# RWKV block inverse with the identity added to its scores; work of the next chunk spread over other levels; a new order at the end of the S5 part

## The reference, cut to what matters

```python
def step(state, inp):                       # wkv7, 8 heads of 64
    r_t, w_t, k_t, v_t, z_t, b_t = inp
    sa = jnp.einsum('bhvk,bhk->bhv', state, z_t)
    state = (state * w_t[:, :, None, :] + sa[..., None] * b_t[:, :, None, :]
             + v_t[..., None] * k_t[:, :, None, :])
    return state, jnp.einsum('bhvk,bhk->bhv', state, r_t)
...
_, _, st_re, st_im = lax.associative_scan(_cplx_op, (a_re, a_im, bu_re, bu_im), axis=1)   # odd_mixer, S5
y = (jnp.einsum('gcn,bsgn->bsgc', C_re, st_re) - jnp.einsum('gcn,bsgn->bsgc', C_im, st_im))
y = jax.nn.gelu(y + D * u)
val, gate = jnp.split(y @ w_glu, 2, axis=-1)
return val * jax.nn.sigmoid(gate)
```

## Time and profile before

| | |
|---|---|
| median of 3 runs | 2760.04 us |
| profiled execution, its own time | 2760.72 us |
| its span | 2758.5 us |
| mean granted TensorE clock | 0.977 |
| TensorE busy | 2622.4 us, 95% of the span, 13567 instructions |
| VectorE, ScalarE, GpSimd busy | 1301.3, 934.0, 879.3 us |
| chain that ended last, by engine | PE 62%, issue 5%, DVE 2%, POOL 2%, ACT 1% |

### The profile page before, as it was taken

How to read it: one execution, slowest core, us unless ns; L and a number is a source line. 1 busy time by engine, 2 the same in 40 slices (tenths; PEclk the granted TensorE clock), 3 DMA queues, 4 the chain that set the end, 5 groups by cost and what they waited for, 6 DMA issues and landing times.

```text
span 2758.5 us, 35785 instructions
## 1 busy us (share of the span) xinstructions
PE 2622.4 (95%) x13567; PEld 2180.1 (79%) x13567; DVE 1301.3 (47%) x1572; ACT 934.0 (34%) x1420; POOL 879.3 (32%) x781
## 2 busy tenths in 40 slices
PE   6999799999799999999999999979999999999998
PEld 4778588888577887888788888868878888888886
DVE  5532277676434556564564435642244413431443
ACT  3442354454433322343343334412233212221333
POOL 4222234333232223575572221222222222222221
PEclk7999899999899999999999999989999999999999
DMA  2111000000012211243251134621111111111112
GB/s 86 44 46 49 20 1 1 1 1 1 13 45 58 58 44 58 64 144 106 65 175 58 46 99 163 202 79 50 47 41 49 50 50 46 49 49 46 49 46 84
DMA packets 239923, 164.57 MB, mean 60 GB/s; under 512 B 23981, under 2 KB 227271, under 8 KB 237767
## 3 DMA queue, kind: packets, MB, share of 16 engines
q1 hardware_dynamic: 225344, 141.37, 17.1%
q10 hardware_dynamic: 14471, 21.74, 2.2%
HBM read 129.51 MB, written 29.36 MB: 58 GB/s over the span
## 4 chain that ended last, share of the span: by engine, by line
PE 62%; issue 5%; DVE 2%; POOL 2%; ACT 1%; DMA 0%; ACTq 0%; SPq 0%; POOLq 0%; DVEq 0%
PE acc_o L1556 53%; PE acc_o L1805 4%; POOL dense_lo L374 1%; PE bank_a L2705 1%; PE bank_b L2728 1%; PE bank_b L2458 1%; PE bank_b L2463 1%; PE bank_a L2449 1%; POOL c_lo L2567 0%; DVE val L2038 0%; PE acc_o L2105 0%; POOL t_gx L2381 0%; POOL t_mg L2374 0%; DVE fine L2222 0%; ACT u_now L2807 0%
## 5 line engine op out<-in xcount | busy, mean ns | idle before, releaser
L374 POOL TENSOR_TENSOR dense_lo<-dense_raw,dense_hi 128x512 fp32r<-128x512 f32 x324 | 427.7, 1320 | 1200.4 <-ACT dense_hi L367 1199.1
L367 ACT CAST dense_hi<-dense_raw 128x512 fp32r<-128x512 f32 x324 | 192.4, 594 | 778.3 <-PE acc_o L1556 719.2
L1556 PE MATMUL acc_o<-a_hi,dense_hi 128*128 128x512 f32 x1328 | 413.9, 393 | 8.2 <-POOL a_lo L2573 4.6
L1556 PE MATMUL acc_o<-a_hi,dense_lo 128*128 128x512 f32 x1328 | 410.7, 391 | 0.0
L1556 PE MATMUL acc_o<-a_lo,dense_hi 128*128 128x512 f32 x1328 | 410.5, 390 | 0.0
L1556 PE MATMUL acc_o<-c_hi,dense_hi 128*128 128x512 f32 x1096 | 340.1, 392 | 22.9 <-POOL dense_lo L374 20.7
L1556 PE MATMUL acc_o<-c_lo,dense_hi 128*128 128x512 f32 x1096 | 338.2, 390 | 0.0
L1556 PE MATMUL acc_o<-c_hi,dense_lo 128*128 128x512 f32 x1096 | 338.1, 390 | 0.0
L1556 PEld LDWEIGHTS acc_o<-a_hi,dense_hi 128*128 128x128 f32 x1328 | 247.2, 189 | 62.1 <-POOL a_lo L2573 5.8
L1556 PEld LDWEIGHTS acc_o<-a_hi,dense_lo 128*128 128x128 f32 x1328 | 250.2, 188 | 52.5
L1556 PEld LDWEIGHTS acc_o<-a_lo,dense_hi 128*128 128x128 f32 x1328 | 250.1, 188 | 52.5
(11 more groups left out here) (382 smaller groups left out, 3776.4 us busy)
## 6 DMA issues: line engine op xcount, KB each, us to landing
dense_raw<-in_f_w_up SPq DMA_DIRECT2D x176, 256.0 KB, 3.0
dense_raw<-in_f_w_down SPq DMA_DIRECT2D x72, 256.0 KB, 2.9
w_raw_e<-in_e_w_in SPq DMA_DIRECT2D x44, 256.0 KB, 2.9
s_states<-t_hx ACTq DMA_DIRECT2D x16, 512.0 KB, 3.0
g_in<-s_inputs SPq DMA_DIRECT2D x8, 1024.0 KB, 5.0
hx<-s_states SPq DMA_DIRECT2D x8, 1024.0 KB, 5.3
dense_raw<-in_o_w_glu SPq DMA_DIRECT2D x32, 256.0 KB, 2.8
s_inputs<-t_in ACTq DMA_DIRECT2D x14, 512.0 KB, 2.7
```

The lines of the kernel that those rows point to most:

```text
L367: nc.scalar.copy(self.hi[:, par, 0:n, :], self.raw[:, par, 0:n, :]).then_inc(w_hi_done, 1)
L374: pool.tensor_tensor(self.lo[:, par, 0:n, :], self.raw[:, par, 0:n, :], self.hi[:, par, 0:n, :].bitcast(F32), op=ALU.subtract).then_inc(w_ ...
L1556: last = nc.tensor.matmul(acc[:, h * HALF:(h + 1) * HALF], w[:, chunk, j, :], x[:, k + j, h * HALF:(h + 1) * HALF], start=first, stop=final)
```

## The change

Part one, the inverse. To the masks of levels 1 to 6 and to `a_zb` the identity is added. A product of (A + I) with X, masked, then has ones on its diagonal, and X times it already contains the old X. The products with the identity (`old`) and the additions (`add_old`) go; VectorE copies group 1 out of PSUM. `a_zb` is now an addition on GpSimd, ahead of `first_pool`.

Part two, the order. `roots_act` becomes `logs_act` behind level 3 and `roots_act` behind level 4; the second pair of exponentials moves behind level 5; `zr_dve` to level 6, `r_dve` behind all levels; `b_pool` ahead of `out_pool`.

Part three, the end of the S5 part. The first six places of the GLU's weights are written out as a table of unit and half; a third unit begins in `bank_a`, which the S5 part no longer needs by then. `states_pe(7)` stands ahead of `output_pe(6)`. All eight `g_part` are on VectorE, four of them ahead of scan 6. Moves of tile 5 are split between SyncE's and ScalarE's queues.

```diff
@@ masks, one instruction
+                    link.run(nc.vector.tensor_tensor(level_mask[:, 1:LEVELS, :], level_mask[:, 1:LEVELS, :],
+                                                     ident[:, :].unsqueeze(1).to_broadcast([P, LEVELS - 1, P]), ALU.add))
@@ close_pe
-                up(add4(banks[g][1], x_inv_t[g], MX_AT[g], None if g else x_inv[g]), f"x_ps{g}")
-                up(add4(banks[g][2], mx[g], XT_AT[g], None if g else x_inv_t[g]), f"x_ps{g}")
+                up(add4(banks[g][1], x_inv_t[g], MX_AT[g]), f"x_ps{g}")
+                up(add4(banks[g][2], mx[g], XT_AT[g]), f"x_ps{g}")
@@ close_dve
-            add_old(c, x_inv[1][:, :, :], banks[1][1], "x1")
+            up(nc.vector.tensor_copy(x_inv[1][:, :, :], psum4(banks[1][1])), "x1")
@@ a_zb
-                up(nc.scalar.copy(a_zb[g][:, :, :], a_b[g][:, :, 0, :]), "a_zb")
+                ptt(pool, a_zb[g][:, :, :], a_b[g][:, :, 0, :],
+                    ident[:, :].unsqueeze(1).to_broadcast([P, RT, CH]), ALU.add, "a_zb")
@@ turn_of_act
-                if k == 3:
+                if k in (3, 4):
+                    half = logs_act if k == 3 else roots_act
...
                 if more and k == 4:
                     exps_act(act, c + 1, 1 - s, 0)
+                if more and k == 5:
                     exps_act(act, c + 1, 1 - s, 1)
@@ S5 end, TensorE
                 states_pe(DT - 2)
-                unit_products(dn, pe, DT, a_hi, a_lo, u_glu, 0, 0, g_ready)
+                pe.wait_ge(unit_free, u_glu + 1)
+                place_products(pe, 0, 0, 2, g_ready)
                 filters_pe(DT - 2)
...
+                states_pe(DT - 1)
+                place_products(pe, 0, 2, 4, g_ready).then_inc(w_used, 1)
                 output_pe(DT - 2)
...
+                place_products(pe, 1, 0, 4, g_ready).then_inc(w_used, 1)
                 filters_pe(DT - 1)
                 output_pe(DT - 1)
...
+                place_products(pe, 2, 0, 4, g_ready).then_inc(w_used, 1)
+                place_products(pe, 3, 4, 8, g_ready).then_inc(w_used, 1)
+                place_products(pe, 4, 4, 8, g_ready).then_inc(w_used, 1)
+                place_products(pe, 5, 4, 8, g_ready).then_inc(w_used, 1)
@@ S5 end, SyncE
                 move_y(sp, DT - 2, (2, 3))
                 move_y(sp, DT - 1, (2, 3))
-                with sp.Fori(1, DT) as i:
+                load_unit(DT + 2)
+                dn.load(sp, w_glu, DT, glu_cols(1, 1), u_glu + 3, 0)
+                with sp.Fori(2, DT) as i:
```

More of the change, by code:

```diff
@@ L952, in grow_pe, with add4 @@
                 up(last, f"mx_ps{g}")
-        def add4(bank, lhs, rhs_at, old=None):
-            if old is not None:
-                units(bank, eye, old, start=True, stop=False)
+        def add4(bank, lhs, rhs_at):
             for i in range(RT):
-                last = beside_zeros(bank, i, lhs[:, i, :], rhs_at + i, start=old is None and i == 0, stop=i == RT - 1)
+                last = beside_zeros(bank, i, lhs[:, i, :], rhs_at + i, start=i == 0, stop=i == RT - 1)
             return last
@@ L2104, in tile_products @@
             for h in range(2):
[L2105 removed]
+                last = nc.tensor.matmul(acc[:, h * HALF:(h + 1) * HALF], w[:, place, j, :],
                                         x[:, k, h * HALF:(h + 1) * HALF], start=first, stop=final)
```

183 lines of the change are left out of this document (110 added, 73 removed).

## The result

| | before | after |
|---|---|---|
| median | 2760.56 us (4 runs, 2758.92 to 2761.87) | 2726.47 us (4 runs, 2726.26 to 2726.75) |
| ratio | | 0.9879, 95% interval 0.9864 to 0.9893 |
| span of the profiled execution | 2758.5 us | 2724.5 us |
| granted TensorE clock | 0.977 | 0.981 |

34.1 us less where 35 was forecast, at 2726.5 for a forecast of 2725. The total hides an error. The table follows the same instructions through the two profiled executions; the lead is what the kernel after has won by then.

A forecast was written before the change was run, and what follows sets the result against it. With TensorE at 95% of the span, its waits and what it executes were the question. RWKV 14.7 plus S5 end 20.5, 35.2 us off 2760.7, gave 2725 on the median; own range 2719 to 2731, 8 in 10 2707 to 2740.

The forecast's parts named there:

- RWKV, what goes: Levels 1 to 6 of a chunk: copies through the identity and waits for roots and z go, 4.3 us per full chunk.
- The collision d: Start of a chunk: GpSimd's a_zb additions and VectorE's first masks exclude each other, costing 2.0 us; bounds 0 and 2.5.
- Chunks 0 and 7: First and last RWKV chunk: levels gain only 2.3 and 2.6 us, less d: 0.3 and 0.6.
- S5, the wait for g_in: Before states 7 TensorE waits from 1791.9 to 1792.6; g_in, issued after four moves, takes 5.0 us to land.
- S5, the two later waits: TensorE idles 3.4 us before the last tile and 2.7 before unit 3, whose weights wait in ScalarE's queue.
- One clock fall, 2.5 us: S5 end: idle lowers TensorE's clock; one fall charged at about 2.5 us, bounds none and two.
- Scan 6: VectorE at the S5 end: with GpSimd silent, scan 6 takes 11 us instead of 19.3.
- No collision: Rival on the first masks: d is 0, RWKV gives 31 us, total 2709; chance 0.22.
- VectorE paces the levels: Rival: the 0.46s are lost to evictions, RWKV gives 0 to 3 us, total 2739; chance 0.15.
- The S5 end gives half, g_in lands late and the clock drops: Rival: g_in later among the moves, both idles drop the clock; 11 us there, total 2734; chance 0.13.
- The slower rival: Clock falls inside RWKV through waits in the levels, for more than one chunk's worth: 2765 to 2800; chance 0.03.
- That the copies had no price: Rival: products may overlap the identity copies, so only the ordering acts; falls together with the second rival, no own chance.

The follow-up runs named there:

- The halves measured alone: Kernel before with only the RWKV parts (inverse and order): 2743.53 us, 16.9 less; with only the new S5 end: 2746.73 us, 13.7 less.
- Experiment 5: Changed kernel with GpSimd's two a_zb additions waiting for VectorE's two first masks instead of the kept scores: 2714.38 us, 12.1 less than the changed kernel.
- experiment 6: Changed kernel with g_in of the last group read ahead of states 6 and the last places' weights in SyncE's queue: 2723.61 us, 2.9 less.
- experiment 8: Changed kernel with the hi part of unit 3's first weights ahead of the first output tile on ScalarE: 2722.23 us, 4.2 less.
- experiment 7: Changed kernel with the last weight loads ahead of the last tile's moves in SyncE's queue: 2726.21 us, against 2726.47.
- experiment 3: Inverse without the new order, S5 end as before, against the kernel before: 2765.6 us, 5.2 slower, ratio 1.0022.
- experiment 9: Changed kernel with the GpSimd wait, g_in first, last weights ahead of moves and unit 3's rounding first, all four: 2704.29 us, 22.2 less.

## Why the prediction was right, and where it was wrong

**The number was right in part by luck.** RWKV gave 14.8 us for 14.7, the S5 end 6.2 less than its 20.5, and 4.9 us that belong to no part of the change filled most of the gap: 2.5 ahead of chunk 0, 0.9 between RWKV and states 6, 1.5 at the sums of the last norm. In the first place the code differs by one more instruction on the masks, in the other two by nothing, and the rows differ by the clock: the four products of L319 at 45 us took 3.75 us before and 2.35 after, three pairs at 1076.8 took 1.06 each before and 0.62 after, the norm's sums 3.42 and 1.91. In the 14 traces chunk 0 begins between 340.80 and 343.94 us, and the changed kernel's is the earliest. The halves measured alone, with less of this luck, gave 16.9 and 13.7. How the executions without a trace divide is not shown.

- *RWKV, what goes (4.3 a chunk).* It was 4.44, all of it in the levels 1 to 6. Step by step, each level counted from its first product or copy, with the forecast in brackets: 0.00 (-0.1), -0.46 (-0.45), -0.47 (-0.45), -1.37 (-1.35), -1.69 (-1.5), -0.45 (-0.4). The chunk period is 47.60 for the 48 named. The level without filler is 3.67, as forecast. VectorE's copy costs what its addition did (a pair takes 1.29 us in both traces).
- *The collision d (2.0).* The mechanism was right and the size nearly: 1.78. Experiment 5 shows it. The row that the prediction gives as s_prev "alone", 2.36 us, is not: GpSimd's 1.58 us on dense_lo began 0.23 us behind it, at 1772.18. Alone the pair takes 1.29 (1774.50 above). The sum of d did not use that row.
- *Chunks 0 and 7.* The net was 2.66 a chunk for 2.3, 16.0 in the six full chunks for 13.8. Chunk 0 gave 0.5 for 0.3. From the scores of chunk 7 to the first product behind RWKV 1.7 us were lost, where the forecast had 0.6 won; 1.5 of that is a clock fall, longer here than in the traces of experiments 6 and 8, which lost 0.2. Two errors of about 2 us each cancel in the 14.8.
- *S5, the wait for g_in (0.7).* **This step failed.** "5.0 us to land" was the page's one figure for eight such reads the earlier trace rows. This one stood behind states 6 and two loads, 1.5 MB, and between the moves. It waited 3.89, and the clock fell: by the end of states 7 TensorE was 6.0 us behind my timeline, nearly all of the 6.2. Experiment 6 shows the cause.
- *S5, the two later waits (3.4 and 2.7).* 2.76 and 2.14, in the places and for the reasons given: the hi part of place 4 ran straight ahead of that of tile 7 (1811.45 and 1811.97), and unit 3's weights stood behind the first output tile; experiments 7 and 8 show both.
- *One clock fall, 2.5 us.* The trace has three, worth about 2.7, 1.3 and 1.6. "The falls seen came after almost 4 us" overlooked one in the trace of before: the norm's sums took 3.42 us (2014.61) behind 2.37 us of idle.
- *Scan 6 (11 us).* 9.8. Most of the difference is the misread pair: freed of GpSimd, s_prev fell from 5.45 to 1.29 us, 2.1 an instruction where the forecast gave back 1.5.

**The rivals.** "No collision" is refuted by the masks at 3.06, and experiment 5, which makes it true, lands 5 us above its 2709: RWKV gave 27.6 us there for 31, as a wait for GpSimd came next, and what stands behind it 19.5 for 20.5 (of which 1.5 are the norm's sums again). "VectorE paces the levels" is refuted for the change (levels at 3.67), but it describes experiment 3: without the new order the copies' worth is lost to other waits, and the collision makes it slower than before. "The S5 end gives half, g_in lands late and the clock drops" had the right mechanism and 0.13; it happened, at 6.2 us less for the 9.5 that I gave it. The slower rival came true in one chunk of eight, not in more than one, which it had set as its point of decision. In the last chunk, which has less beside its first levels, TensorE waits 1.41 for a_k and 1.11 for `rounded`, and the clock fell:

```profile
680.00:690.00 10.00, 8.89 (x47) 8.21 (x46) 5.39 (x9) 2.05 (x4) 0.72 (x1) 0.66 0.00 0
```

Its level 1 took 5.62 us where experiment 9, at a clock of 1.00 there, has 3.95; the chunks 0 to 6 with the same kind of waits kept a clock of 1.00. The trace of the inverse alone has such a fall in a full chunk too (0.76). That the copies had no price is refuted as well: the order alone stays 0.54 us a chunk above the change, in spite of the change's collision of 1.78, so that with the new order the copies were worth 2.3.

## What to carry to other kernels

The page's one figure for a kind of transfer is not the price of the one transfer that stands in the queue behind 1.5 MB of others: add up what is issued ahead of it and read the DMA share of that stretch. When an operation is moved to GpSimd, ask what VectorE does in that very microsecond with operands in SBUF; here it was worth a third of the change to let GpSimd wait for two masks of VectorE (2714.4), and with the waits of the S5 end reordered as well the same work takes 2702, 58 us under the kernel before where the change had 34. Judge an edit of 2 to 3 us by its own rows too, since a clock fall elsewhere in the program can hide it; and before a difference between two traces is booked to a part of the code, compare the same instruction at both ends of that part: of the 18.2 us won by states 6 here, 3.4 lay outside RWKV.
